# Router from raw transposed sums, context work as filler, dummy products in the first loads, and both blocks' norms in one step

## The reference

```
h = rmsnorm(x, attn_norm);  proj = h @ w_in
x = x + concat(attention, delta rule) @ w_out
h = rmsnorm(x, ffn_norm)
group_logits = h @ w_group;  expert_logits = h @ w_router      # 4 groups of 8 experts
# top group, then top 2 experts in it; weights from softmax
x = x + sum over chosen experts of weight * (silu(h @ w_gate) * (h @ w_up)) @ w_down
x = rmsnorm(x, final_norm)
```

```
mod = silu(c) @ w_mod + b_mod      # for the tokens and, with c_ctx, for the context
h  = rmsnorm(x, norm1_g) * (1 + sc1) + sh1;   hc = the same of ctx
q, k, v of h and hc = h @ w_in_2, hc @ w_in_2;  head norms; two kinds of attention, one with
   a position bias rpb;  x = x + g1 * merge @ w_out_2
x = x + g2 * swiglu(rmsnorm(x, norm2_g) * (1 + sc2) + sh2)
```

## Time and profile before

| | us |
|---|---|
| median of 3 runs | 930.96 (930.38 to 934.65) |
| the profiled execution | 934.39 |
| its span, first to last instruction | 932.5 |
| PE busy | 841.4 (90%) |
| PE weight loads busy | 567.2 (61%) |
| DVE, ACT, POOL busy | 383.4, 257.9, 51.3 |
| HBM read | 206.73 MB |

### The profile page before, as it was taken

The page is one execution under the profiler, slowest core; times in us unless marked ns, Lnnn a source line. Parts: engine busy times, 40 slices in busy tenths (PEclk is TensorE's granted clock), DMA queues, the critical chain, the costliest instruction groups (busy, mean ns, idle before and its releaser), DMA issues.

```text
span 932.5 us, 12507 instructions
## 1 busy us (share of the span) xinstructions
PE 841.4 (90%) x5093; PEld 567.2 (61%) x5093; DVE 383.4 (41%) x709; ACT 257.9 (28%) x416; POOL 51.3 (5%) x36
## 2 busy tenths in 40 slices
PE   5999999989989877777777789999999999999998
PEld 4876768766455443332333245458875688888886
DVE  1358134535233111111011136673333766675765
ACT  2143223331020221221112030125463343333431
POOL 1000032101000000000000005210000000000000
PEclk9999999989988998988897799999999999999999
DMA  8762446558385899999999995350000743554601
GB/s 322 272 226 91 138 169 234 181 181 316 111 301 219 327 409 409 409 409 409 409 409 409 406 336 188 112 178 1 2 1 1 255 149 137 204 202 143 218 1 45
DMA packets 117835, 208.39 MB, mean 223 GB/s; under 512 B 7554, under 2 KB 34459, under 8 KB 117667
## 3 DMA queue, kind: packets, MB, share of 16 engines
q1 hardware_dynamic: 114914, 203.51, 59.2%
q10 hardware_dynamic: 2816, 4.27, 1.4%
q0 software_dynamic: 64, 0.05, 0.0%
HBM read 206.73 MB, written 1.08 MB: 223 GB/s over the span
## 4 chain that ended last, share of the span: by engine, by line
PE 76%; DMA 11%; DVE 4%; issue 3%; SPq 2%; ACT 1%; ACTq 1%; POOL 1%; DVEq 0%; PEld 0%; PEldq 0%; POOLq 0%
DMA arena<-in_w_down_dram 10%; PE psa L488 8%; PE psa L867 7%; PE psv L1039 4%; PE psa L1039 4%; PE psv L825 4%; PE psa L937 3%; PE psx L962 3%; PE psa L809 3%; PE psa L755 2%; PE psa L724 2%; PE psv L1040 2%; PE psa L1040 2%; PE psx L516 2%; PE psv L498 2%
## 5 line engine op out<-in xcount | busy, mean ns | idle before, releaser
L2010 DVE TENSOR_TENSOR unit_parts<-ring,unit_parts 128x2048 fp32r<-128x2048 f32 x33 | 75.5, 2289 | 59.2 <-ACT unit_parts L1444 59.2
L1444 ACT ACTIVATE unit_parts<-ring 128x2048 fp32r<-128x2048 f32 x33 | 63.2, 1914 | 74.8 <-PE psa L1040 43.8
L867 PE MATMUL psa<-ring,arena 128*128 128x512 f32 (+1 forms) x192 | 76.1, 557 | 2.0 <-DVE arena L1509 1.2
L825 PE MATMUL psv<-ring,arena 128*32 128x256 f32 x1024 | 59.4, 381 | 19.9 <-DMA ring<-in_w_up_dram 15.5
L488 PE MATMUL psa<-arena,ring 128*128 128x256 f32 x320 | 72.1, 388 | 1.0 <-DVE arena L1507 1.0
L1039 PE MATMUL psv<-column_parts,unit_parts 128*128 128x512 f32 (+1 forms) x192 | 67.0, 396 | 2.5 <-DVE arena L2037 1.4
L488 PEld LDWEIGHTS psa<-arena,ring 128*128 128x128 f32 x320 | 62.2, 195 | 11.1 <-DVE arena L1507 1.3
L1039 PE MATMUL psa<-column_parts,unit_parts 128*128 128x512 f32 (+1 forms) x192 | 65.2, 388 | 0.0
L867 PEld LDWEIGHTS psa<-ring,arena 128*128 128x128 f32 x192 | 36.3, 190 | 41.1 <-issue 37.3
L825 PEld LDWEIGHTS psv<-ring,arena 128*32 128x32 f32 x1024 | 32.2, 110 | 45.1 <-DMA ring<-in_w_up_dram 21.3
L1040 PE MATMUL psv<-column_parts,unit_parts 128*128 128x256 f32 (+1 forms) x192 | 52.8, 275 | 0.0
(11 more groups left out here) (355 smaller groups left out, 1393.3 us busy)
## 6 DMA issues: line engine op xcount, KB each, us to landing
ring<-in_w_gate_dram SPq DMA_DIRECT2D x43, 1024.0 KB, 9.2
ring<-in_w_up_dram SPq DMA_DIRECT2D x43, 1024.0 KB, 5.2
arena<-in_w_down_dram SPq DMA_DIRECT2D x32, 1024.0 KB
ring<-in_w_in_dram SPq DMA_DIRECT2D x28, 1024.0 KB, 9.5
ring<-in_w_mod_dram SPq DMA_DIRECT2D x24, 1024.0 KB, 7.1
ring<-in_w_down_dram SPq DMA_DIRECT2D x11, 1024.0 KB, 7.3
ring<-in_w_out_dram SPq DMA_DIRECT2D x8, 1024.0 KB, 6.0
arena<-rpb_pad ACTq DMA_DIRECT2D x4, 512.0 KB, 16.7
```

The costliest lines, as they stand in the source:

```text
L825: mm = pe.matmul(mG[32 * e:32 * e + 32, f0:f0 + FF], XT[:, 2 * pair + kk, 32 * e:32 * e + 32], w[:, e, kk * FF:(kk + 1) * FF], start=(pair ...
L867: mm = pe.matmul(bank[:, 0:ncols], lhs[:, k, b * P:(b + 1) * P], units[k // per][:, k % per, :], start=(k == 0), stop=(k == KD - 1))
L1444: act.activation(unit_parts[q % 3][:, 0, :], slot_of(NPRE + u_), ACT.Copy).then_inc(upper_done, 1)
L2010: vec.tensor_tensor(lo, slot_of(NPRE + at["mlp"] + 3 * n + kind), hi, ALU.subtract).then_inc(lower_done, 1)
```

## The change

- *Start*: once csil is zeroed, PE runs 7 products of zeros (32 weight columns, 256 moving), and 6 more behind the transpose of the gain rows. POOL does the first `power` before it touches the bias.
- *Router*: w_group and w_router are loaded in natural chunk order and scaled on DVE by ffn_norm (now one more row of `rows`). PE transposes the raw sums xres pair by pair into xT, the first two pairs between the third and the fourth output sum, and multiplies them by the scaled wr in two halves into two banks (`route`). DVE scales the logits by the norm's factor. h2 is made after the trip count, and is no longer transposed. The context's transposes go all to ACT's banks; two of them, the modulation products and one block of `ctx_cols(0)` stand before the counts; the other block, the modulation sums and all of `ctx_cols(1)` behind. The parts of the two last modulation tiles lie in another place (`mixed_mp`).
- *Hand-over*: DVE multiplies xres by final_norm (xgain) while ACT squares xres; ACT squares xgain. One power of four columns gives both norms: the first factor r, and (r^-2 * EPS + mean of xgain squared)^-1/2 for hnx from xgain. ACT issues the bias transfers after its four squares. xres itself is scaled behind the transposes' copies.

```diff
+                for _ in range(n):
+                    pe.matmul(PSX[1][0:32, 0:KD * 32], csil[:, 0, :], csil.rearrange("p k c -> p (k c)"), start=True, stop=True)
+            pe.wait_ge(csil_ready, 1)
+            keep_busy(7)
...
+            keep_busy(6)
             pe.wait_ge(rows_normed, 1)
...
+            route_banks = (PSX[1], PSA[(na + 2) % 3])
+            at["route"] = route_banks
+            def route(k0, k1):
+                for b in range(NB):
+                    for k in range(k0, k1):
+                        mm = pe.matmul(route_banks[b][:, 0:NR], xT[:, k, b * P:(b + 1) * P], wr[:, k, :],
+                                       start=(k == 0), stop=(k == KD - 1))
+                    if k1 == KD:
+                        mm.then_inc(logits_ready, 1)
+            pe.wait_ge(out_sum_added, NB)
+            for kp in range(2):
+                turn_pair(xres, kp, v_bank()).then_inc(v_ready, 1)
             project(out_units[1], 3, 0, KD)
+            pe.wait_ge(v_free, nv)
+            pe.wait_ge(out_sum_added, NB + 1)
+            pe.wait_ge(route_gained, 1)
+            route(0, 4)
+            pe.wait_ge(out_sum_added, 2 * NB)
+            for kp in range(2, 4):
+                turn_pair(xres, kp, v_bank()).then_inc(v_ready, 1)
...
             pe.wait_ge(rows_normed, 2)
-            pe.wait_ge(out_sum_added, 2 * NB)
-            turn(hnc)
-            hc_at = nv
-            mod_tiles(MOD_MIXED)
-            pe.wait_ge(v_free, hc_at)
...
+            pe.wait_ge(v_free, nv)
+            route(4, KD)
+            pe.wait_ge(logits_taken, NB)
+            turn_pair(hnc, 2, a_bank()).then_inc(a_ready, 1)
+            turn_pair(hnc, 3, a_bank()).then_inc(a_ready, 1)
+            mod_products(MOD_MIXED[0])
+            mod_products(MOD_MIXED[1])
             pe.wait_ge(a_free, na)
-            ctx_cols(0, unit(1), 256)
...
-            pe.wait_ge(rows_normed, 3)
-            turn(h2)
-            pe.wait_ge(v_free, nv)
-            pe.wait_ge(a_free, na)
-            pe.wait_ge(s_wr, 32)
-            bank = v_bank()
-            for b in range(NB):
...
-            kb_units = unit(2)
-            ctx_cols(1, kb_units, 512, (0,))
+            ka_units = unit(1)
+            ctx_cols(0, ka_units, 256, (0,))
             sel = rt[:, 0:NB * NE].rearrange("p (b e) -> p b e", b=NB)
             pe.wait_ge(chosen_done, 1)
...
-            ctx_cols(1, kb_units, 512, (1,))
+            ctx_cols(0, ka_units, 256, (1,))
+            mod_sums(MOD_MIXED[0])
+            mod_sums(MOD_MIXED[1])
+            ctx_cols(1, unit(2), 512)
+            pe.wait_ge(rows_normed, 3)
...
+                              ("ffn", v("ffn_norm").rearrange("l (c p) -> (l c) p", p=P))):
...
+            sp.dma_start(wr[:, :, 0:NG], v("w_group").rearrange("l (k p) g -> p (l k) g", p=P)).then_inc(s_wr, 16)
+            sp.dma_start(wr[:, :, NG:NR], v("w_router").rearrange("l (k p) g -> p (l k) g", p=P)).then_inc(s_wr, 16)
...
             act.wait_ge(out_sum_added, 2 * NB)
+            squares(xres, h2)
             act.dma_start(ffn_bc, v("ffn_norm").broadcast_to((P, D))).then_inc(s_ffn_bc, 16)
             act.dma_start(fin_bc, v("final_norm").unsqueeze(0).broadcast_to((P, D))).then_inc(s_fin_bc, 16)
-            squares(xres, h2)
-            turned(hTc, modA[:, 1, :], modT[:, 0:KD, 1])
-            for n in MOD_MIXED:
-                x_mod(n)
-            act.wait_ge(s_pad2, 16)
+            turned(hTc, modA[:, 1, :], modT[:, 0:KD, 1], pairs=range(KD // 2))
...
-            a_out([cA[:, b, :] for b in range(NB)])
-            turned(h2T)
...
+            for n in MOD_MIXED:
+                x_mod(n)
+            act.wait_ge(s_pad2, 16)
+            a_out([cA[:, b, :] for b in range(NB)])
...
             act.wait_ge(moe_sums_added, 4 * trips + 1)
+            squares(xres, hnx)
+            for b in range(NB):
+                act.wait_ge(gained, b + 1)
+                act.activation(sqg[:, b, :], xgain[:, b, :], ACT.Square,
+                               accum_out=both_ss[:, 2 + b:3 + b]).then_inc(squares_done, 1)
             act.wait_ge(s_pad2, 16)
...
-            squares(xres, hnx)
-            act.wait_ge(first_block_done, NB)
-            squares(xres, hnx)
             a_out([cB[:, b, 512:1024] for b in range(NB)])
             turned(hTx, modA[:, 0, :], modT[:, 0:KD, 0])
+            act.wait_ge(first_block_done, NB)
...
+            dve.wait_ge(s_wr, 32)
+            vec.tensor_tensor(wr[:], wr[:], vc[:, ROWS["ffn"]:ROWS["ffn"] + KD].unsqueeze(2).broadcast_to((P, KD, NR)),
+                              ALU.mult).then_inc(route_gained, 1)
...
-            dve.wait_ge(out_sum_added, 2 * NB)
-            turned(hTc, modA[:, 1, :], modT[:, 0:KD, 1])
-            dve.wait_ge(s_ffn_bc, 16)
-            normed(xres, h2, gain=ffn_bc, apart=KD)
-            for n in MOD_MIXED:
-                mod_cols(n)
-            turned(h2T)
+                if b == NB - 1:
+                    for kp in (2 * half, 2 * half + 1):
+                        bank = v_take()
+                        vec.tensor_copy(xT[:, 2 * kp:2 * kp + 2, :],
+                                        bank[:].rearrange("p (k t) -> p k t", k=2)).then_inc(v_free, 1)
+            nsq += 2
+            dve.wait_ge(squares_done, nsq)
+            rsqrt(ss, rstd, D)
...
-            bank = v_take()
-            vec.tensor_copy(lg[:], bank[:, 0:NB * NR].rearrange("p (b n) -> p b n", b=NB)).then_inc(v_free, 1)
-            dve.wait_ge(v_free, nv)
+            for b in range(NB):
+                dve.wait_ge(logits_ready, b + 1)
+                vec.tensor_scalar(lg[:, b, :], at["route"][b][:, 0:NR], rstd[:, b:b + 1], None, ALU.mult).then_inc(logits_taken, 1)
+            dve.wait_ge(logits_taken, NB)
...
-            for r in range(ROUNDS):
-                vec.tensor_scalar(posall[:, :, r * NE:(r + 1) * NE], pos[:], -1.0 - SLOTS * r, None, ALU.add)
-                vec.tensor_copy(comball[:, :, r * NE:(r + 1) * NE], comb.rearrange("p b g e -> p b (g e)"))
...
             link(vec.tensor_scalar(trips_i[:, 0:1], cmax, float(SLOTS - 1), None, ALU.add))
...
+            dve.wait_ge(s_ffn_bc, 16)
+            for b in range(NB):
+                ins = vec.scalar_tensor_tensor(h2[:, b, :].rearrange("p (k j) -> p k j", k=KD), every(xres[:, b, :], KD),
+                                               rstd[:, b:b + 1], every(ffn_bc, KD), ALU.mult, ALU.mult)
+            ins.then_inc(rows_normed, 1)
+            for n in MOD_MIXED:
+                mod_cols(n)
+            for r in range(ROUNDS):
+                vec.tensor_scalar(posall[:, :, r * NE:(r + 1) * NE], pos[:], -1.0 - SLOTS * r, None, ALU.add)
+                ins = vec.tensor_copy(comball[:, :, r * NE:(r + 1) * NE], comb.rearrange("p b g e -> p b (g e)"))
+            link(ins)
...
-            normed(xres, xres, gain=fin_bc, own=True)
+            for b in range(NB):
+                vec.tensor_tensor(xgain[:, b, :], xres[:, b, :], fin_bc, ALU.mult).then_inc(gained, 1)
+            nsq += 4
+            dve.wait_ge(squares_done, nsq)
+            dve.wait_ge(gained, NB)
+            link(vec.tensor_scalar(both_rstd[:, 0:2], both_ss[:, 0:2], 1.0 / D, EPS, ALU.mult, ALU.add))
+            link(vec.tensor_scalar(both_ss[:, 2:4], both_ss[:, 2:4], 1.0 / D, None, ALU.mult))
+            vec.scalar_tensor_tensor(both_rstd[:, 2:4], both_rstd[:, 0:2], EPS, both_ss[:, 2:4],
+                                     ALU.mult, ALU.add).then_inc(power_req, 1)
+            nrs += 1
+            dve.wait_ge(power_done, nrs)
+            for b in range(NB):
+                ins = vec.tensor_scalar(hnx[:, b, :], xgain[:, b, :], both_rstd[:, 2 + b:3 + b], None, ALU.mult)
+            ins.then_inc(rows_normed, 1)
+            turned(hTx, modA[:, 0, :], modT[:, 0:KD, 0])
+            for b in range(NB):
+                vec.tensor_scalar(xres[:, b, :], xgain[:, b, :], both_rstd[:, b:b + 1], None,
+                                  ALU.mult).then_inc(first_block_done, 1)
             dve.wait_ge(first_block_done, NB)
-            normed(xres, hnx)
-            turned(hTx, modA[:, 0, :], modT[:, 0:KD, 0])
...
+            pool.wait_ge(s_ident, 16)
+            power(rstd)
             pool.wait_ge(s_pad0, 1)
...
-            pool.wait_ge(s_ident, 16)
-            power(rstd)
...
-            power(rstd)
-            power(rstd)
+            power(both_rstd)
             pool.wait_ge(s_bias_rows, 64)
```

More of the change, by code:

```diff
@@ L228, in two_blocks @@
         hnx = ar(4096, NB, D)
+        xgain, sqg = ar(8192, NB, D), ar(10240, NB, D)
         onat = ar(4096, NB, D)
@@ L530, in mod_sums @@
                     bank = v_bank()
-                    pe.matmul(bank[:], c("sumrow"), mp[:, n % 2, :], start=True, stop=True).then_inc(v_ready, 1)
+                    pe.matmul(bank[:], c("sumrow"), mod_part(n), start=True, stop=True).then_inc(v_ready, 1)
                 at["mod", n] = nv
@@ L1202, in squares, with turned @@
```

(22 more changed lines are left out.)

41 lines of the change are left out of this document (23 added, 18 removed).

## The result

The changed kernel takes 921.76 us (median of four runs, 919.43 to 923.49) against 930.67 beside it, 8.9 us less; the ratio is 0.9884, with a 95% interval of 0.9856 to 0.9911 (8.3 to 13.4 us less). The forecast was 922.2. The profiled execution took 921.78 us, with a span of 920.0; that of the kernel before took 934.39, with 932.5.

The account below looks back on a forecast made before the run. PE bounds it outside the transfer-bound expert loop (408 GB/s), with start, router and hand-over to price. Terms -4.9 - 9.1 + 5.2 = -8.8 us, from the median 930.96 to 922.2 us; range 914.5 to 929.5.

Parts of the forecast that it names:

- the term of 4.9 us: Start: 2.6 us from earlier first products plus 2.3 us of low clock avoided, 4.9 us less.
- Rival (a): Start: the filler of 32 columns doesn't raise the clock, start +2.0 us, 929.1 us in all; chance 0.26.
- the 11.9 counted without a fall: Router: new order ends at 290.2 instead of 302.06 us, 11.9 us less before any clock loss.
- The 2.8 us: Router: taken back for one clock fall behind narrow products and transposes, leaving 9.1 us less.
- rival (e): Router: no clock fall, PE keeps the high clock through its short products, 919.4 us in all; chance 0.18.
- the step to the loop's first product: Between router and expert loop: the step to the loop's first product stays 3.0 us.
- (d): Expert loop: changed rounding moves a token's expert, four more trips, near 1045 us; chance 0.02 with anything unforeseen its size.
- +5.2 forecast: Hand-over: joint norms cost 5.2 us more, from late copies and a low clock; ends 1.1 less, 6.5 more.
- the 2.1 us on PE: Hand-over: PE's projections start at 553.9 instead of 556.0 us, 2.1 us gained on PE.
- The first, 3.3 us: Hand-over: bias lands 4.4 us later, so DVE's first of ten copies starts at 621.6 instead of 618.33, 3.3 us lost.
- the 1.9 us for a low clock: Hand-over: PE idles near 4.5 us, so its last seven transposed banks and first scores run slow, 1.9 us.
- Rival (b): Hand-over: the bias lands in time, its queue having less before it, 915.9 us in all; chance 0.16.

Follow-up runs that it names:

- e1: The changed kernel without its 13 dummy products at the start, POOL's new order kept; 923.28 us, ratio 0.989 to the kernel before.
- e7: The kernel before with the start's part alone (13 dummy products, POOL's power first); 929.1 us, ratio 0.9961 to the kernel before.
- e4: The changed kernel with all 32 router products in one run behind all transposes; 922.76 us, ratio 0.9887 to the kernel before.
- e5: The kernel before with nine dummy products filling PE's 4.13 us idle gap in the router; 932.52 us, ratio 0.9998 to the kernel before.
- e8: The changed kernel itself, unchanged, run again as the measure for the other runs; 921.55 us, ratio 0.9886 to the kernel before.
- e3: The changed kernel with six dummy products behind the last context product ahead of the expert loop; 918.89 us, ratio 0.9848 to the kernel before.
- e2: The changed kernel with POOL serving three head-norm powers before waiting for the bias and adding masks; 922.18 us, ratio 0.9883 to the kernel before.
- e10: The changed kernel with mask additions moved from POOL to DVE and six dummy products ahead of the expert loop; 914.43 us, ratio 0.9793.

## Why the prediction came right, step by step

**The start held.** The forecast had the first product at 12.8 us and 64 instructions near 14; they are 12.59 and 14.05, and the term of 4.9 us is 5.0 at the end of the first group. Rival (a), that dummies of 32 columns don't raise the clock, is refuted by the transposes and first products of the changed kernel beside those of e1. What I took for granted, that the shift is kept whole to the end, is the weak step: e7 gives 3.6 us and allows 5.0, e1 gives hardly any.

**The router was under-sized, for the clock.** The order of work came out nearly as counted: 11.69 us in the trace against the 11.9 counted without a fall. The 2.8 us that I took off for one fall behind the narrow products were wrong; rival (e) had it: none of the eleven traces of the new order has a low stretch there. I had read the earlier trace rows as narrow products that lower the clock of a busy engine. e4 runs all 32 in one piece without a fall, and e7 runs them in the order of before without one. (The terms up to the 261.1 of the prediction make 260.9; nothing hangs on it.) The Trainium skill's rule of the same part (the clock falls on idle time) fits e5's first stretch and, in the router, all traces of the new order, which have no wait over 0.83 us up to the last context product. It doesn't by itself explain the stretch that stayed in e5.

About half of the router's gain is the clock's. The order of before has 61.97 us with two low stretches and 58.8 to 59.0 with one (e7, e5), so some 56 without any; the new order has 50.3. That last step is an extrapolation, not a run.

**The loop's start was missed.** I let the step to the loop's first product stand at 3.0 us and gave it no fall. It idles 3.14 us, the clock fell in most traces, and the loop's gates come 1.6 us later for it.

**The loop** kept eight trips, which refutes (d). Its length scatters from 225.7 to 229.1 us over 14 traces with its code unchanged; the +1.24 of the balance is within that.

**The joint norms were over-sized**: +5.2 forecast, +2.2 from the first trace to the second, about 0.5 in the mean of five traces each, 2.7 +- 2.9 in the runs. Their chain was the right one: late bias, mask on POOL, DVE's powers behind it, PE idle before its transposes; and the 2.1 us on PE came as 2.3. Both terms of the 5.2 were too large. The first, 3.3 us, came from bias transfers issued behind four squares, 4.4 us later. The first went out at 524.37, right behind DVE's second product with the gain (it ends at 524.3), which is the last thing that ACT's list waits for ahead of it; the third square (524.06, 1.04 us) still ran and the fourth had not begun. So the last was issued 4.5 us after the loop's end instead of 2.1, 2.4 us later and not 4.4. It landed 23.3 us after its issue (23.0 before), so that part of the reasoning held, and DVE's copies begin 82.9 us after the loop instead of 81.6: 1.3 us, not 3.3. The second is the 1.9 us for a low clock behind PE's idle time. The low stretch came where it was forecast, but cost 0.9 us from the copies to the scores (6.5 against 5.6). Whether it comes is chance once more: e8 has it, e1, e3 and e4 haven't; e2, which idled 4.47 us there, had one of twice the length. Rival (b), bias in time, fell too: it is 2.7 us late.

That the time was met to half a us is luck. Between the two profiled executions the router was off by -2.6 us, the norms by -3.0, the low stretches before S by -1.0; the loop's start gave back 1.6 and the loop 1.2. In all these executions differ by 12.5 us, 3.7 more than the forecast sum of 8.8. The medians differ by 8.9 only because that of the kernel before, 930.67, stands 3.7 us under its own profiled run, while that of the changed kernel doesn't. The ratios, 0.9884 and 0.9886 in e8, stand for 10.6 to 10.8 us, about 2 us more than the sum.

## What to carry to other kernels

Work moved to POOL is off DVE's path only while DVE idles: here a mask placed "later" on POOL went on stopping DVE, and moving it into DVE's own waiting time paid. Where PE must wait a few us ahead of dense work, dummy products in exactly that gap kept the clock and delayed nothing (e3, e10); whether the whole kernel gains has to be measured, for e3 was 3.5 us faster and e5 not at all. And look at a low stretch of the clock in more than one trace before giving it a cause and a price.

## What the runs showed of the hardware that was not expected

- While POOL ran a 128x2048 addition of 3.81 us, operations of DVE took 3.77 us (128x16, else 0.17) and 4.29 us (128x512, else 0.69). The Trainium skill (SBUF — State Buffer, section SBUF: two separate sides) says that the two engines share a pair of ports, which some forms of DVE's operations need, those with two inputs in SBUF among them, and which one operation holds to its end; these traces agree.
- With the same code, low stretches of the clock came near 60 us in six traces of nine and not in three, and the second output sum moved over 4.0 us. A run of 32 products of 36 columns went with a fall in two traces of the same order and without one in a third.
- ACT's queue issued a transfer at 524.37 us while a square that stands before it, begun at 524.06, still ran for 0.7 us, and before the next square, which also stands before it, began at 525.10. In this trace the transfer was late by the waits ahead of it and not by the squares.
- From 605.30 us on PE ran nothing but transposes, behind 3.43 us of idle time, and the clock rose at 609.0 us among them (0.51 from 606 to 609 us, 1.00 from 609.2 to 610); e8 and e2 show the same. The prediction had cited transposes as not counting as busy work for the clock in the same way; these rows disagree.
